# Strassen passes in place of three square products ahead of a feed-forward that already uses them

## What is computed

```python
ya = jnp.einsum('bse,ed->bsd', oa, w_proj_a[l])        # 1024 x 1024 by 1024 x 1024
yb = jnp.einsum('bse,ed->bsd', ob, w_proj_b[l])        # the same size
g = jax.nn.sigmoid(gate_pre).reshape(B, S, 2, D_MODEL)
merged = g[:, :, 0] * ya + g[:, :, 1] * yb
h = h + jnp.einsum('bsd,de->bse', merged, w_out[l])    # the same size
hn = rms_norm(h, norm_ffn_w[l])
u = jax.nn.relu(jnp.einsum('bsd,df->bsf', hn, w_ff1[l]))   # 1024 -> 4096
h = h + jnp.einsum('bsf,fd->bsd', u * u, w_ff2[l])         # 4096 -> 1024
return rms_norm(h, final_norm_w)
```

## Time and profile before

| | us |
|---|---|
| median of 3 runs | 1883.43 |
| the profiled execution | 1883.48 |
| its span, first to last instruction | 1881.3 |
| TensorE busy | 1871.9 |
| VectorE, ScalarE, GpSimd busy | 1183.4, 949.5, 329.8 |
| end of the gate round (first matmul of branch A) | about 990 |
| output product, from its first matmul | about 1163 |
| first pass of the feed-forward | 1252.1 |

### The profile page before, as it was taken

How to read it: one execution, slowest core, us unless ns; L and a number is a source line. 1 busy time by engine, 2 the same in 40 slices (tenths; PEclk the granted TensorE clock), 3 DMA queues, 4 the chain that set the end, 5 groups by cost and what they waited for, 6 DMA issues and landing times.

```text
span 1881.3 us, 26892 instructions
## 1 busy us (share of the span) xinstructions
PE 1871.9 (100%) x9832; PEld 1606.0 (85%) x9832; DVE 1183.4 (63%) x1621; ACT 949.5 (50%) x1541; POOL 329.8 (18%) x182
## 2 busy tenths in 40 slices
PE   9999999999999999999999999999999999999998
PEld 6989898989898989888888888888888888888887
DVE  7675858585767676544311122787868778688774
ACT  5455655556565656445333232236676585333343
POOL 1202020211111111132224444420000000021002
PEclk9999999999999999999999999999999999999999
DMA  6351515151514242432254444557668587464312
GB/s 222 100 171 56 192 57 195 51 199 51 181 64 158 84 159 89 162 120 77 73 185 146 151 135 173 182 182 268 233 236 286 192 284 255 168 227 153 151 74 90
DMA packets 103283, 293.19 MB, mean 156 GB/s; under 512 B 10888, under 2 KB 27912, under 8 KB 92192
## 3 DMA queue, kind: packets, MB, share of 16 engines
q1 hardware_dynamic: 100896, 283.69, 43.5%
q10 hardware_dynamic: 2304, 8.39, 1.1%
HBM read 204.94 MB, written 87.10 MB: 155 GB/s over the span
## 4 chain that ended last, share of the span: by engine, by line
PE 99%; DVE 1%; POOL 0%; DVEq 0%; issue 0%; POOLq 0%
PE gp L755 14%; PE gp L753 14%; PE gp L754 14%; PE scores L1025 6%; PE scores L1027 6%; PE scores L1029 6%; PE gp L773 3%; PE gp L771 3%; PE gp L772 3%; PE gp L1025 2%; PE gp L1027 2%; PE gp L1029 2%; PE scores L871 2%; PE scores L870 2%; PE ob L918 2%; PE ob L919 2%
## 5 line engine op out<-in xcount | busy, mean ns | idle before, releaser
L753 PE MATMUL gp<-r1h,w_hi 128*128 128x512 f32 x880 | 346.7, 394 | 0.0
L755 PE MATMUL gp<-r1h,w_lo 128*128 128x512 f32 x880 | 343.7, 391 | 0.0
L754 PE MATMUL gp<-r1l,w_hi 128*128 128x512 f32 x880 | 342.8, 390 | 0.0
L1025 PE MATMUL scores<-xh,qh 128*128 128x512 f32 x512 | 199.7, 390 | 0.1
L1029 PE MATMUL scores<-xh,ql 128*128 128x512 f32 x512 | 199.2, 389 | 0.0
L1027 PE MATMUL scores<-xl,qh 128*128 128x512 f32 x512 | 199.2, 389 | 0.0
L755 PEld LDWEIGHTS gp<-r1h,w_lo 128*128 128x128 f32 x880 | 165.2, 188 | 35.1
L753 PEld LDWEIGHTS gp<-r1h,w_hi 128*128 128x128 f32 x880 | 165.4, 188 | 32.9
L754 PEld LDWEIGHTS gp<-r1l,w_hi 128*128 128x128 f32 x880 | 165.4, 188 | 32.6
L2077 POOL TENSOR_TENSOR w_lo<-w_raw,w_hi 128x1024 fp32r<-128x1024 f32 x25 | 60.6, 2423 | 490.6 <-ACT w_hi L1128 467.1
L773 PE MATMUL gp<-w_hi_pair,r1l 128*128 128x256 f32 x512 | 144.8, 283 | 0.0
(11 more groups left out here) (346 smaller groups left out, 4250.7 us busy)
## 6 DMA issues: line engine op xcount, KB each, us to landing
xraw<-xo_d SPq DMA_DIRECT2D x54, 1024.0 KB, 5.1
w_raw<-in_in_blocks SPq DMA_DIRECT2D x64, 512.0 KB, 3.7
proj_d<-ev SPq DMA_DIRECT2D x128, 256.0 KB, 2.4
rq<-in_ff_quarters SPq DMA_DIRECT2D x32, 1024.0 KB, 7.8
xo_d<-res SPq DMA_DIRECT2D x78, 256.0 KB, 3.4
xo_d<-ring SPq DMA_DIRECT2D x60, 256.0 KB, 3.5
gt<-proj_d SPq DMA_DIRECT2D x32, 256.0 KB, 3.7
xt<-in_x_halves SPq DMA_DIRECT2D x8, 512.0 KB, 7.1
```

The costliest lines, as they stand in the source:

```text
L753: pe.matmul(gp[half][:], wh[slot][:, k, :], mh[:, k, t], start=(k == 0), stop=False)
L754: pe.matmul(gp[half][:], wh[slot][:, k, :], ml[:, k, t], start=False, stop=False)
L755: mm = pe.matmul(gp[half][:], wl[slot][:, k, :], mh[:, k, t], start=False, stop=(k == KT - 1))
L1025: pe.matmul(bank, qh[s % 3][:, k, cols], xh[s % 3][:, k, :], start=first and k == 0, stop=False, skip_group_check=True)
```

## The change

The two projections and the output product become three groups of seven passes, in one stream ahead of the feed-forward's eight: groups PA, PB, WO, then F1 (4) and F2 (4), 77 passes. Passes are counted from 0, so PA is 0 to 6, PB 7 to 13, WO 14 to 20 and F1 begins at 21.

- Removed: the 24 plain blocks with their weight splits, the staging of oa and ob, and the sums for the first feed-forward group beside the output product.
- Gate round: SP loads quarters of oa and ob, GpSimd builds the four sums of each (`turn_item`, 24 subtractions of 128x512, six items in slots 4, 5, 8, 9, 12, 13), SP stores them; the last item of each is VectorE's (`turn_late`).
- The ring slot of a pass is (s+1) % 3, so passes 0 and 1 have slots that the gate round's input does not occupy.
- GpSimd makes the low q parts of passes 3 to 23 (`POOL_LOW`); before and behind that they are VectorE's.
- In PA and PB the output tiles of passes 1, 5 and 6 are added by VectorE and multiplied by the gate on GpSimd (`gated`); those of pass 4 are multiplied by VectorE from PSUM (`gated_bank`). In PB VectorE then adds the two branches (`merged`).
- The last merged quarter, C12, is complete after pass 13. At pass 14 VectorE builds from it the sums for WO: T3, T2, T1, T4 (`wide_sums`, `narrow_sum`, `last_sum`); T3, T4, T1 and B22 are stored and read back, B11, B21 and T2 are taken from SBUF.
- WO: VectorE adds x from PSUM (`residual`), and the token scale is taken in passes 17 to 20 (`first_square` behind bank 1 of pass 17 and bank 3 of pass 19, `token_var`, `token_root`, `root`), each half from its first tile of features. At pass 21 VectorE scales C22 and C12 and builds the sums of F1.
- Behind pass 25 the feed-forward is as before.

Core of the diff:

```diff
-            for b in range(KT):
-                for i in range(2):
-                    unit(N_PA + b, b % 2, i, r2h, r2l, ...)
...
             def stage_unit(s, u, between=None):
                 g, idx = divmod(s, NP)
+                at = (s + 1) % 3
                 if u == 0:
-                    pe.wait_ge(p_lo, 2 * s + 2)
+                    pe.wait_ge(q_low, s + 1)
+                    pe.wait_ge(xq_low, s + 1)
...
+                    if s == S_WO + 3 and u == 1:
+                        first_square(0)
+                    if s == S_WO + 5 and u == 3:
+                        pe.wait_ge(ev_a, a_out(G_WO, 4, 0))
+                        first_square(1)
```

ScalarE's turn of pass s:

```diff
+                if s + 2 < STAGES:
+                    q_hi_part(s + 2)
+                    if s == S_F1:
+                        for n in range(3 * UN, 4 * UN):
+                            square(n)
+                    if s == S_F1 + 1:
+                        hidden(s)
+                    x_hi_part(s + 2)
+                if g < G_WO:
+                    ...
+                    for n in {2: (4, 5), 4: (6, 7, 8, 9), 5: (10, 11, 12, 13), 6: (14, 15)}.get(idx, ()):
+                        gate_sigmoid(16 * g + n)
+                    projected(s)
+                if g == G_WO:
+                    if idx == 3:
+                        square(3)
+                        token_root(0)
+                    if idx == 6:
+                        token_root(1)
+                    for n in {2: (0, 1, 2), 5: (4, 5, 6, 7, 8), 6: (9, 10, 11)}.get(idx, ()):
+                        square(n)
```

VectorE's turn of pass s:

```diff
+                elif s == S_WO:
+                    for u in range(UN):
+                        merged(C12, u)
+                        dve.wait_ge(m_done, 3 * UN + u + 1)
+                        wide_sums(0, u, res[:, u, HALF:], xraw[1][:, u, :])
+                    for u in range(UN):
+                        narrow_sum(0, u, res[:, u, HALF:])
+                    x_lo_part(s + 2)
+                    for u in range(UN):
+                        last_sum(0, u, xraw[1][:, u, :], tb[:, u, :])
+                elif s == S_F1:
+                    for u in range(UN):
+                        scaled(C22, u)
+                    for u in range(UN):
+                        scaled(C12, u)
+                    ...
+                elif s in (S_WO + 1, S_F1 + 1):
+                    weight_sum(g, 3)
+                    if s + 2 > POOL_LOW[-1]:
+                        q_lo_first(s + 2)
+                    for u in range(UN):
+                        add_bank(s, u)
+                    x_lo_part(s + 2)
+                elif g == G_WO:
+                    if idx == 4:
+                        x_lo_part(s + 2)
+                        root(0)
+                        for u in range(UN):
+                            scaled(C11, u)
+                    ...
+                if g == G_WO and idx in SET_A:
+                    for u in range(UN):
+                        residual(s, u)
+                    if idx == 3:
+                        token_var(0)
```

GpSimd:

```diff
+            def q_lo_part(s):
+                at = (s + 1) % 3
+                if s == POOL_LOW[0]:
+                    pool.wait_ge(q_low, s)
+                pool.wait_ge(p_hi, 2 * s + 1)
+                pool.tensor_tensor(ql[at][:], quarter_of(s)[:], qh[at][:].bitcast(F32), ALU.subtract).then_inc(q_low, 1)
...
+            for s in range(STAGES):
+                g, idx = divmod(s, NP)
+                if s + 2 in POOL_LOW:
+                    q_lo_part(s + 2)
+                if g < G_WO and idx in (1, 5, 6):
+                    for u in range(UN):
+                        gated(g, {1: C11, 5: C22, 6: C12}[idx], u)
+                if S_WO <= s <= S_F1:
+                    for n in {3: range(1, 4), 5: range(4, 8), 6: range(9, 12), 7: range(12, 16)}.get(s - S_WO, ()):
+                        square_sum(n)
```

More of the change, by code:

```diff
@@ L580, in _ @@
+                if j == 14:
+                    for second in range(2):
+                        turned_stores(late[second], bt_done, 4 * second, second, UN - 1)
+                    sp.wait_ge(st[0], 16 * (N_GATE + UN))
+                    for n in range(UN):
+                        gate_load_tile(n)
+                    quarter_load(0, 3)
             for k in range(2):
                 store(N_PA - 2 + k)
+            sp.wait_ge(gemm_done, 2 * N_PA)
+            quarter_load(0, 2)
+            x_quarter_load(2)
@@ new lines, in gate_sigmoid @@
+            def gate_sigmoid(n):
+                act.wait_ge(g_in[n % GT], 16 * (n // GT) + 16)
+                act.activation(gts[n % GT], gts[n % GT], ACT.Sigmoid).then_inc(g_sig, 1)
+            for j in range(12, 16):
+                n = N_GATE + j
+                if j < 15:
+                    split_hi(n + 1, (n + 1) // 2, (n + 1) % 2)
+                for i in range(2):
+                    evac(n, i)
+                    if j == 15 and i == 0:
+                        x_hi_part(0)
+                if j == 14:
+                    q_hi_part(0)
@@ new lines, in merged @@
+            def merged(c, u):
+                k, half = tile_of(c, u)
+                to = res[:, k, half * HALF:(half + 1) * HALF]
+                if c == C21:
+                    dve.wait_ge(ev_a, a_out(G_PB, 4, u))
+                    src = gts[gate_tile(G_PB, C21, u) % GT]
+                else:
+                    dve.wait_ge(g_used, pool_gated(G_PB, c, u))
+                    src = (ta if c == C12 else tb)[:, u, :]
+                dve.tensor_tensor(to, to, src, ALU.add).then_inc(m_done, 1)
@@ new lines, in _ @@
+                    if g == G_PB and idx in (2, 6):
+                        for u in range(UN):
+                            merged(C11 if idx == 2 else C22, u)
+                if g == G_WO and idx in SET_A:
+                    for u in range(UN):
+                        residual(s, u)
+                    if idx == 3:
+                        token_var(0)
+                elif g in (G_PA, G_PB) and idx == 4:
+                    for u in range(UN):
+                        gated_bank(s, u)
+                    for u in range(UN if g else 0):
+                        merged(C21, u)
+                elif (g > G_F2 or idx in (1, 5, 6)) and s not in (S_WO + 1, S_F1 + 1):
@@ L2049, in _ @@
                         add_bank(s, u)
+                        if s == S_F1 - 1 and u == 1:
+                            root(1)
                         if s == STAGES - 2 and u == 1:
```

951 lines of the change are left out of this document (504 added, 447 removed).

## The result

The changed kernel takes **1907.86 us** (median of 4 runs, 1907.65 to 1908.45) against 1883.45 us for the kernel before on the same chip, a ratio of 1.013 (95% interval 1.0113 to 1.0148): slower by 24.4 us. The forecast of 1893 us lay too low, and so did the whole range of 1858 to 1903 us. The profiled execution took 1907.66 us, with a span of 1905.9.

The account below looks back on a forecast made before the run. TensorE's instructions were taken to set the time: 1883.48 us profiled less 32.6 for removed matmuls gives 1850.9, plus 43 of stalls 1893.9, taken as 1893 us. Range 1858 to 1903 us.

Parts of the forecast that it names:

- TensorE's columns: Whole stream: 1152 matmuls removed and 1008 added, 144 fewer at 0.2267 us each, 32.6 us less.
- the large stalls: TensorE's waits at passes 16, 17, 20 and 23: 12, 9, 7 and 11 us.
- Pass 23: Wait before this pass: VectorE's chain from pass 19's first bank sum, with GpSimd's share, gives 11 us (1.5 to 19).
- The main case: Stream stalls of 33 to 53 us, giving 1884 to 1904 us; chance 0.48.
- rival 3: TensorE's clock falls in the four long stalls, 3.1 us lost each, up to 12.6: 1905 us; chance 0.07.
- the gate round: Before the stream: 24 GpSimd subtractions and 8 MB each way, costed at nothing, 0 to 8 us if the cover failed.
- Rival 1: In the stream GpSimd's work falls into VectorE's waits without colliding; stalls total 7 us, 1858 us; chance 0.27.
- The lower bounds: Stalls without GpSimd's share at passes 13, 16, 17, 20, 23, 25: 0, 0, 3.5, 1, 1.5, 1 us.
- Rival 2: In the stream half the collisions of VectorE and GpSimd bite: stalls of 18 to 28 us, 1874 us; chance 0.15.
- Rival 4: DMA is the bound in WO: loads half a pass late, 5 us, 1898; held in the main range, no own chance.

Follow-up runs that it names:

- run 1: Changed kernel with all low weight parts back on VectorE, none on GpSimd: 1890.45 us.
- run 2: run 1 with GpSimd's gatings and sums of squares also left out, so its time is only a bound: 1879.69 us.
- run 4: Separate small kernel, not the layer: VectorE and GpSimd work beside each other on separate tiles in seven phases; 264.11 us in a single execution.
- run 10: run 9 with the low weight parts of passes 3 to 23 back on GpSimd, as in the changed kernel: 1892.20 us.
- run 11: run 9 without GpSimd's gatings and sums of squares: 1865.67 us.
- Run 5: Changed kernel with one border reordered: ScalarE's copies of passes 21 and 23 earlier, VectorE's low part for pass 24 ahead of pass 22's banks: 1904.96 us.
- Run 12: Separate kernel, none of the layer: TensorE's matmul blocks with pauses of varied length between them; 680.75 us in a single execution.
- Run 8: Changed kernel with only the issue of the stream's first loads changed, spread among the gate round's stores: 1903.47 us.
- run 9: Changed kernel with all low weight parts on VectorE, first loads spread, and work reordered around the output product and first feed-forward border: 1874.89 us.

## Why the prediction was wrong

**What held.** TensorE's columns: 32.6 us, with passes of 10.88. The place of the large stalls: they stand before passes 13, 16, 17 and 23, ended by VectorE's sums or ScalarE's copies, and in the last unit of pass 19, ended by ScalarE's square. Their cause, for the 17 us of the low parts and the 9 to 11 us of GpSimd's other work: runs 1, 2, 4, 10 and 11. And their sum: 43 us forecast, 41.0 measured. That the sum fits so well is partly luck. Single terms were off by up to 3.5 us, in both directions, and 2.9 us stand where none was forecast:

| pass | forecast | measured wait |
|---|---|---|
| 13 | 2 | 2.0 |
| 16 | 12 | 8.8 |
| 17 | 9 | 6.4 |
| 20 | 7 | 6.5 (in pass 19's last unit, for the square) |
| 23 | 11 | 14.5 |
| 25 | 2 | 0 |
| 6, 21, 24 | none | 0.8, 1.5, 0.6 |

Pass 23 is the largest miss among them. I priced GpSimd's share there at 10 of 23.9 us; the four scalings of C22 alone took 10.3 us in place of the 2.6 that I had, and behind them the copies of pass 21 waited for the last sums, a wait that I had not followed. Run 5 shows that this wait and the place of the copies made 7 of the 14.5 us. So the term came near 11 us with the wrong parts in it.

**What failed, first: the clock.** The main case had it at nothing and put it into rival 3, with a chance of 0.07, because "mostly it falls into time in which operands are late anyway". That argument doesn't hold. The slow matmuls come after the wait, when operands are there and the next pass's bank already depends on them. Run 12 gives the price without the kernel around it, 1.3 to 2.7 us for nearly every pause of 3.25 us or more. Rival 3's own price, 3.1 for each of four stalls, was a little high; the trace shows 8.9 us in the stream. The warning in the page TensorE: Matmul & The Clock Gate of the Trainium skill (Part 1, HAM oscillation), which I had quoted and set aside, was right here: in the trace each of the four long waits is followed by a slow stretch. At run 12's price four such stalls cost 5 to 11 us beside their length, and a term of that size belonged in the sum.

**Second: the gate round.** It was costed at nothing, 0 to 8, with GpSimd's idle time as cover. The subtractions did stay hidden, but the DMA queue did not: 5.7 us of wait and 1.7 us of slow clock came from loads issued ahead of a store whose landing frees ScalarE's buffer, whose copy frees TensorE's bank. I had written that "loads would then land later"; the store behind the loads was the link that I left out. Run 8 takes both away. That the gain then shrinks from 7.8 to 4.4 us is shown; that it went into the waits at passes 2 and 4 is read from its trace, a late load for pass 2 and the crossing of the two engines for pass 4. The order of run 9, with pass 2's load moved ahead and the low parts on VectorE, has neither wait.

The forecast's own sum was 1893.9. With 8.9 for the clock in the stream and 7.4 for the gate round, and less the 2.0 us by which the stalls were forecast too high, it is 1908.2, against 1907.66 profiled.

**The rivals.** Rival 1, that the pair does not collide, was given 0.27. The durations of the changed kernel refute it, and so does the 65 us reading of run 1. From 1100 to 1180 us VectorE is busy for 77.6 of 80 us and GpSimd for 47.4, with VectorE's waits for GpSimd inside its busy time: GpSimd's work did not fall into gaps, it lengthened VectorE's instructions. The lower bounds behind rival 1 were too low as well, as far as run 2 can tell: with nothing on GpSimd but with the low parts on VectorE it took 1879.7 us, passes 17 and 23 waited 5.7 us each where the bounds had 3.5 and 1.5, and 8.7 us of slow clock came on top. A kernel with the low parts on GpSimd and no collisions can't be run, so 1858 itself stays untested. Rival 2, at 1874 us, did not come true; that run 9 ends there, with the low parts on VectorE and other orders, is a coincidence. Rival 4 shows only in small, as 1 to 4 us of VectorE's idle time before x parts and rows of x.

**What stays open.** Run 9's 11.3 us before pass 23 could perhaps shrink by moving VectorE's work to ScalarE, which is busy for 53% of that run; that wasn't tried. Why one pause costs 1.3 us of slow clock and the next 2.7, and why one of 2 us costs something and the next nothing, is not explained by any run.

## What to carry to other kernels

Where both read SBUF, add GpSimd's work to that of VectorE's instructions with two SBUF inputs, as if they ran on one engine. Take their durations alone and not the busy time of a trace, which holds their waits for each other. If the sum comes near the length of the stage, moving an instruction from VectorE to GpSimd makes it longer: here 21 of them cost the kernel 17 us, in both orders tried. Price a stall of TensorE as its length and a part for the clock that does not grow with it, 1.3 to 2.7 us here for nearly all pauses from 3.25 us on, so that two short waits can cost more than one long one. And when loads are moved ahead in a queue, follow the stores behind them to the buffer that they free.

## What the runs showed of the hardware

- A VectorE instruction with two SBUF inputs and a GpSimd instruction take turns: 2.28 us become 6.58 and 0.68 become 4.98 beside GpSimd's 4.46. The exclusion takes in a tensor_scalar with one SBUF input (0.41 us alone, up to 4.7 beside GpSimd), but neither a PSUM input (0.68 in both cases) nor the reciprocal (3.29 in both).
- A step in the price of pauses: nothing at 0.9 and 2.0 us, 1.3 to 2.7 us from 3.25 to 12.9, with one pause of 3.25 us free of charge. In the kernels four of nine waits of 1.84 to 2.19 us were followed by 1.7 us of slow clock.
- At the lower level the matmuls of 512 columns start 0.43 us apart, against 0.2267.
- An engine's busy time holds its waits for the other engine, so it can fall when work is given to it: VectorE's by 17.2 us with 21 instructions more.
